# A hybrid encoder layer on one core: the ratio of the softmax sums moves from VectorE to GpSimd, and VectorE's combination between its two bias operations

## What is computed

```python
s = jnp.einsum('bqhcd,bkhcd->bhcqk', qblk, kf) + bias[None, :, None]
pr = jax.nn.softmax(s, axis=-1)
w = pr[:, :, 0] - lam * pr[:, :, 1]
return jnp.einsum('bhqk,bkhe->bqhe', w, vf)
```

## Time and profile before

| | us |
|---|---|
| median of 3 runs | 1035.57 (1035.33 to 1035.8) |
| the profiled execution, whole | 1035.5 |
| its span in the profile | 1033.7 |
| TensorE busy | 1003.1 (97%) |
| VectorE busy | 655.1 (63%) |
| ScalarE busy | 580.7 (56%) |
| GpSimd busy | 496.4 (48%) |
| mean granted clock of TensorE | 0.998 |

### The profile page before, as it was taken

One profiled execution on the slowest core, in us unless ns is written; L12 is line 12 of the kernel. 1 busy time (PEld: TensorE's weight loads), 2 busy tenths in 40 slices (PEclk: granted clock), 3 DMA queues, 4 the chain that ended last, 5 costly groups with the idle time before them and its releaser, 6 DMA issues.

```text
span 1033.7 us, 15465 instructions
## 1 busy us (share of the span) xinstructions
PE 1003.1 (97%) x5792; PEld 796.5 (77%) x5792; DVE 655.1 (63%) x1055; ACT 580.7 (56%) x890; POOL 496.4 (48%) x404
## 2 busy tenths in 40 slices
PE   7999999999999999979999999999899999999997
PEld 6877777777788888857777777777788888888886
DVE  4654948493583350379999999999965344445423
ACT  7738485845641231379999999999842221112112
POOL 1233243626567440056677677666676344353421
PEclk9999999999999999999999999999999999999999
DMA  9651543323265538659687487343384222432321
GB/s 339 245 171 36 173 147 103 117 82 133 62 184 168 158 86 217 204 139 248 164 203 205 107 208 192 93 130 124 114 279 148 87 87 99 148 100 87 107 81 41
DMA packets 105929, 150.34 MB, mean 145 GB/s; under 512 B 10232, under 2 KB 68728, under 8 KB 105848
## 3 DMA queue, kind: packets, MB, share of 16 engines
q1 hardware_dynamic: 105712, 149.36, 48.0%
q10 hardware_dynamic: 144, 0.00, 0.0%
HBM read 102.07 MB, written 44.11 MB: 141 GB/s over the span
## 4 chain that ended last, share of the span: by engine, by line
PE 75%; DVE 16%; issue 7%; ACT 1%; DMA 1%; SPq 0%; DVEq 0%; POOLq 0%; POOL 0%; ACTq 0%
DVE E_ L1643 11%; PE b_ps L1819 6%; PE b_ps L1922 6%; PE b_ps L1924 6%; PE b_ps L1923 6%; PE b_ps L1821 6%; PE b_ps L1820 6%; PE g_ps L1819 4%; PE g_ps L1821 4%; PE g_ps L1820 4%; PE o_ps L1985 3%; PE w_ps L1968 2%; PE h_ps L1819 2%; PE uT_ps L1873 2%; PE h_ps L1821 2%
## 5 line engine op out<-in xcount | busy, mean ns | idle before, releaser
L1254 ACT ACTIVATE E_<-E_,nmax 128x1024 f32<-128x1024 f32 (+1 forms) x184 | 186.7, 1018 | 14.9 <-DVE nmax L1643 14.7
L1643 DVE CUSTOM_DVE_ANT_0 E_<-s_ps,bias 128x1024 f32<-128x1024 f32 (+1 forms) x184 | 188.0, 1057 | 3.6 <-PE s_ps L1935 3.6
L972 POOL TENSOR_TENSOR E_<-E_,ratio 128x576 f32<-128x576 f32 (+3 forms) x92 | 84.5, 918 | 85.8 <-DVE E_ L1659 85.8
L1821 PE MATMUL b_ps<-u_hi,wA_lo 128*128 128x512 f32 x288 | 112.3, 390 | 0.0
L975 POOL TENSOR_TENSOR E_<-E_ 128x576 f32<-128x576 f32 (+3 forms) x92 | 103.7, 1127 | 7.2
L1935 PE MATMUL s_ps<-KL,QL 128*128 128x512 f32 x256 | 90.7, 435 | 13.8 <-DVE nmax L1643 13.0
L1819 PE MATMUL b_ps<-u_hi,wA_hi 128*128 128x512 f32 x240 | 95.4, 398 | 4.0 <-DVE u_lo L1413 3.4
L1820 PE MATMUL b_ps<-u_lo,wA_hi 128*128 128x512 f32 x240 | 93.5, 390 | 0.0
L1968 PE MATMUL w_ps<-ident,E_ 128*128 128x128 f32 x624 | 83.5, 273 | 1.7 <-ACT WT L1285 1.7
L1285 ACT ACTIVATE WT<-w_ps 128x1024 f32<-128x1024 f32 (+1 forms) x96 | 83.4, 868 | 2.8 <-PE w_ps L1968 2.6
L1968 PEld LDWEIGHTS w_ps<-ident,E_ 128*128 128x128 f32 x624 | 72.6, 140 | 14.8 <-issue 3.8
(11 more groups left out here) (228 smaller groups left out, 2316.4 us busy)
## 6 DMA issues: line engine op xcount, KB each, us to landing
QL<-qk_t SPq DMA_DIRECT2D x32, 256.0 KB, 6.8
KL<-qk_t SPq DMA_DIRECT2D x32, 256.0 KB, 8.2
bias<-line_d SPq DMA_DIRECT2D x8, 960.0 KB, 11.7
x_sb<-in_x SPq DMA_DIRECT2D x12, 512.0 KB, 9.0
z_ch<-z_stage SPq DMA_DIRECT2D x24, 256.0 KB, 2.5
qk_t<-qh SPq DMA_DIRECT2D x24, 256.0 KB, 2.3
qk_t<-ql SPq DMA_DIRECT2D x24, 256.0 KB, 2.8
mf<-mix_t SPq DMA_DIRECT2D x24, 256.0 KB, 4.0
```

The source lines that it names most:

```text
L1254: act.activation(e, e, ACT.Exp, bias=nmax[:, n % 5, c:c + 1], scale=-1.0, accum_out=sums[:, n % 5, c:c + 1]).then_inc(e_done, 1)
L1643: dve.tensor_tensor_reduce(weights_at(n)[:, c, 0:n_tok], s_ps[:, c, 0:n_tok], b[:, ::-1], -1.0, 3e38, ALU.add, ALU.min, nmax[:, n % 5, c:c ...
L1821: mm = pe.matmul(dst, sl, mh, start=False, stop=k == n - 1)
```

## The change

The ratio is computed by GpSimd, ahead of its own combination (share); VectorE's factor keeps only the reciprocals. GpSimd's multiplication takes the ratio as a scalar of each partition and so has one input tensor. VectorE issues the first bias operation of step n + 4 before its combination of step n + 2, and the second behind it. The split goes from 448 to 512 columns (long, long) and from 768 to 704 (long, short), so that GpSimd has 512 and 320.

```diff
-            return {(1, 1): 448, (1, 0): 768, (0, 0): 256, (0, 1): 128}[(int(long_now), int(long_next))]
+            return {(1, 1): 512, (1, 0): 704, (0, 0): 256, (0, 1): 128}[(int(long_now), int(long_next))]
...
+            def share(n):
+                gp.wait_ge(r_done, n + 1)
+                if n >= 4:
+                    gp.wait_ge(w_dve, n - 3)
+                    gp.wait_ge(scaled, n - 3)
+                gp.tensor_scalar(ratio[:, n % 4:n % 4 + 1], sums[:, n % 5, 0:1], rsum[:, n % 24, 1:2], neglam[:],
+                                 ALU.mult, ALU.mult).then_inc(rr_done, 1)
+
             def combine(n):
                 n_tok = UNITS[STEPS[n][2]][0]
                 one, two = (weights_at(n)[:, c, split_at(n):n_tok] for c in range(2))
                 gp.wait_ge(w_dve, n + 1)
-                gp.tensor_tensor(two, two, ratio[:, n % 4:n % 4 + 1].to_broadcast([P, n_tok - split_at(n)]),
-                                 ALU.mult).then_inc(scaled, 1)
+                gp.tensor_scalar(two, two, ratio[:, n % 4:n % 4 + 1], None, ALU.mult).then_inc(scaled, 1)
                 gp.wait_ge(scaled, n + 1)
                 gp.tensor_tensor(one, one, two, ALU.add).then_inc(w_gp, 1)
...
             for n in range(NSTEP):
                 blk, head, u, qt = STEPS[n]
+                share(n)
                 combine(n)
...
             def factor(n):
                 dve.wait_ge(e_done, 2 * n + 2)
                 dve.reciprocal(rsum[:, n % 24, :], sums[:, n % 5, :]).then_inc(r_done, 1)
-                dve.wait_ge(r_done, n + 1)
-                if n >= 4:
-                    dve.wait_ge(w_gp, n - 3)
-                dve.scalar_tensor_tensor(out=ratio[:, n % 4:n % 4 + 1], in0=sums[:, n % 5, 0:1],
-                                         scalar=rsum[:, n % 24, 1:2], in1=neglam[:], op0=ALU.mult, op1=ALU.mult
-                                         ).then_inc(rr_done, 1)
...
                 if n + 2 < NSTEP:
                     factor(n + 2)
+                if n + 4 < NSTEP:
+                    biased(n + 4, 0)
+                if n + 2 < NSTEP:
                     combine(n + 2)
                 if n + 4 < NSTEP:
-                    biased(n + 4, 0)
                     biased(n + 4, 1)
```

## The result

| | before | after |
|---|---|---|
| median, us | 1035.66 | 1085.89 (1084.59 to 1086.52) |
| ratio to before | | 1.0481, 95% interval 1.0468 to 1.0495 |
| span in the profile, us | 1033.7 | 1083.6 |
| GpSimd busy, us | 496.4 | 560.4 |
| VectorE busy, us | 655.1 | 627.3 |

Both medians are of four runs. The forecast was 1029.6 us, with a range of 1026.0 to 1036.5. The change costs 50.2 us instead. The page after: engine totals, the slices that answer to the earlier trace rows with ScalarE's beside them, and the chain's shares.

The account below looks back on a forecast made before the run. The attention loop was taken as bound by the 3.47 us ring of combination, GpSimd's multiplication, addition and ratio. Gains 10.3 − 1.9 − 2.0 = 6.4 us, taken as 6.0: 1035.5 − 6.0 + 0.1 = 1029.6 us, range 1026.0 to 1036.5.

Parts of the forecast that it names:

- Multiplication with one tensor input (m): GpSimd's multiplication by the ratio at 512 columns: 0.68 us, bounds 0.60 and 1.04.
- m + s: GpSimd's multiplication plus its ratio (s, 0.34 us): bounds 0.79 to 1.64 us, giving a ring of 3.02 to 3.87.
- The ring: Long-step cycle of combination, GpSimd's multiplication, addition, ratio: 3.25 us instead of 3.47, gaining 10.3 us over 47 steps.
- the block ends: Last two long steps of a block: 2.87 us against 2.60, at most 3.8 us on 14 steps, 1.9 taken.
- the short steps: Short steps at 256 columns: 2.2 us against 2.07, at most 1.8 us on 14 steps; nothing taken.
- the weight parts: GpSimd's 1.28 us low parts of an output weight delay the ratio: 0.5 us a head, 2 us lost in four heads.
- the lead of two steps: VectorE's combination runs two steps ahead of its reader: covers about half the block-end loss and the 256-column short-step loss.
- Ratio off VectorE, and its block: VectorE's ratio is blocked until GpSimd's addition ends, 0.35 us against 0.22; moving it removes the block and 93 instructions.
- Ratio on GpSimd: New one-element operation on GpSimd, ahead of its multiplication's next use: 0.34 us, bounds 0.19 and 0.60.
- The order covers the handover: First bias operation, ahead of the combination, covers VectorE's wait for the ratio; without it a step costs 3.25 + 1.14.
- The slower rival: GpSimd's ring is too long, seen in VectorE's wait for the ratio; at the present multiplication rate about 1047 us; chance 0.16.
- The middle rival: Gain taken back, or 1.14 ns a column makes the multiplication 0.77 us, ring 3.34; either ends near 1034; chance 0.20.

Follow-up runs that it names:

- Experiment 2: Kernel before with only GpSimd's multiplication changed to the one-input form; ratio, order and split as before: 1067.48 us, ratio 1.0302.
- experiment 11: Kernel before with only GpSimd's multiplication changed, to one input and two operations; ratio on VectorE, order and split as before: 1031.63 us, ratio 0.9961.
- experiment 7: Changed kernel with two-input multiplication, split 640/832/320, next ratio ahead of the weight part, and VectorE's old order (combination before both biases): 1059.69 us, ratio 1.0234.
- experiment 1: Changed kernel with only GpSimd's multiplication put back to the two-input form: 1047.93 us, ratio 1.0116.
- Experiment 8: Changed kernel with a second operation, times 1.0, added to GpSimd's multiplication: 1033.10 us, ratio 0.9976.
- experiment 4: Kernel before with single GpSimd instructions added behind its last one, at 512 and 256 columns: one operation 1.56 to 1.58 us, two 0.62 at 512.
- experiment 9: Changed kernel with multiplication's second operation, times 1.0, and the next ratio computed ahead of the output weight's low part: 1031.19 us, ratio 0.9957.

## Why the prediction was wrong

**The step that failed** is the part "Multiplication with one tensor input (m)". I took m(512) = 0.68 us, with bounds 0.60 and 1.04. It measured 1.56. I had taken the two-input form as the upper bound, on the view that reading one tensor less cannot be slower, and the rate from a select over 128 columns. The select is another operation. Nothing in the trace showed a one-operation multiplication of any width: the forecast said so and still closed the range with it. 1.56 + 0.34 = 1.90 for m + s lies beyond the 1.64 that was the upper end.

**What that did.** The ring is 2.23 + m + s = 4.13 us by the forecast's own formula; the trace has 4.12 to 4.16. By the table the long steps cost 26.6 us, the short ones 12.1, the block ends 11.6 and the last 0.5: 50.8 us between the first and the last combination, of 50.2 in the whole time. For the short steps and the weight parts together the forecast had 2 us, on the ground that the lead of two steps covers them.

**A reading that was off.** The forecast took 3.47 us for each of the 47 long steps. That is the most frequent interval before, but the mean is 3.57: where heads_scaled (0.69 and 0.42 us) stands on VectorE, a step takes 3.94 and 3.67. In the changed kernel this work falls into VectorE's wait and the step is 4.14 there as well. Hence 26.6 us and not 47 × (4.14 − 3.47) = 31.5.

**Ratio off VectorE, and its block: right.** Experiment 2 lengthens the block to 0.95, experiment 11 removes it. **Ratio on GpSimd: right**, 0.342 us against 0.34. **Addition: right**, 1.286 against 1.29. **VectorE's combination: right**, 752 ns at 512 columns against 752 by the slope. **The order covers the handover: right**, experiment 7. These sizes were read off rows of the same or a near form; the multiplication had no such row.

**The slower rival** had its place right: the ring decides, and the cost is VectorE's wait for the ratio. It was priced at the present rate, 1047 us, and experiment 1 measured 1047.9 for that case. That agreement is luck in its terms: 6.6 us were put on the long steps and 1.8 came, 3.2 on the block ends and 6.4 came, 2 on the weight parts and 5.4 came in the short steps. It had 0.16 and should have had a case above it. The middle rival has a slip: 1.14 ns a column makes m = 0.77 only without the 0.075 for the tile operand that m = 0.68 includes. With it m is 0.85, the ring 3.42 and the 2.3 us gained are less than the 3.9 lost.

**What the right m would have given.** Experiment 8 is the forecast's kernel with m = 0.69. It gained 2.6 us, not 6.0. The long steps gave 11.0 us where 10.3 were forecast. The losses were put too low. The block ends cost 4.1: the 704-column steps take 2.90 us (628.77 to 631.67), 0.30 over before, and I had halved the loss to 1.9 on the strength of the two-step lead. The short steps cost 5.2 where I had nothing for them and 2.0 for the weight parts. Of these 5.2 the weight parts are about 3.3: a head with them takes 38.60 us and one without 37.46 (the head from 678.16), 1.14 more, against 38.30 − 37.99 = 0.31 before, so 0.83 a head and not 0.5. 11.0 − 4.1 − 5.2 = 1.7 us, and the loop is 1.7 shorter; the remaining 0.9 of the 2.6 lies outside it and is not explained. So the second step of the prediction that failed is the cover by the lead of two steps, which took half of one loss and all of another to be hidden.

The Trainium skill's figure ("GPSIMD Engine Reference", section "Elementwise — side-by-side cycle accounting", 769 ns for 512 elements as best case) would have given a gain of 2.2 us by the forecast's sum. That this is near the 2.6 is chance, as m was 0.69 and the losses larger. The only multiplication here of that length is the one with two column operands (0.77 us). Two operations with constants took 0.62, less than that best case, and one operation 1.56, for which the section gives no figure; the measurements decide.

## What to carry to other kernels

When a change puts in a form of instruction that the trace does not hold, its cost has no upper bound from "it does less": time it alone at the real width first, and leave the range open until then. Where two engines alternate on one tile, write the ring down (each instruction and handover once round): here it gave 3.61, 4.04, 3.27 and 3.34 us for kernels that measured 3.61, 4.07, 3.28 and 3.34. Take the mean of the steps and not a typical one when a gain is multiplied out. And a lead of two steps is no reason to cost a longer ring at half or at nothing: here 3.9 us of losses were forecast, and 9.3 came.

## What the runs showed of the hardware that I had not expected

On GpSimd, fp32, 512 columns: a one-input instruction with one arithmetic operation took 1.56 to 1.58 us, with two 0.62 (0.77 with two column operands), a copy 0.61, a two-input one 1.26, and 1.04 where the second input is one column spread (experiment 4). In the kernel, times 1.0 as a second operation took 1560 ns to 692. A two-input VectorE instruction over a single element lasted 0.22 us beside an idle GpSimd and 0.95 behind a running addition, to whose end it was held (experiment 2). A combination of 128 columns, 0.35 us otherwise, was held to 1.35 by a weight part on GpSimd (experiment 9).
